# State steps by halves, gate products between them, and a product of two identities behind every half step

## The reference, cut to what matters

```python
# rwkv_branch(z_in, s0_f, s0_b, lp): two directions d over the same tokens
for d in range(2):
    w = -softplus(-(rw_w0[d] + tanh(w_lo) @ rw_w2[d])) - 0.5
    decay = to_heads(exp(-exp(w)))
    a = to_heads(sigmoid(rw_a0[d] + a_lo @ rw_a2[d]))
    kd = kh * (1.0 + (a - 1.0) * k_a)
    y, s_fin = wkv7_scan(rh, decay, kd, vh, -kk, kk * a, s0[d], reverse=(d == 1))
o = ys[0] + ys[1]
o = (o - mean(o)) * rsqrt(var(o) + GN_EPS) * gn_g + gn_b
o = o + bonus[0] + bonus[1]          # then times silu(rw_g)

# gmlp_mix: per chunk of 128 tokens and head
vh = layernorm(gelu(v)) * ln_g + ln_b
mixed = einsum('gpq,bnqgc->bnpgc', w_s, vc) + b_s
out = gelu(u) * mixed                # then times silu(gm_g)

# adaLN: the gate part of mod is needed at the very end only
mod = silu(c) @ ada_w + ada_b;  shift, scale, gate = split(mod, 3)
# attention: rpb is a table of relative position biases, padded into HBM
```

## Time and profile before

| what | value |
|---|---|
| median of 3 runs | 2621.25 us (2617.14 to 2621.5) |
| the profiled execution, its own time | 2618.64 us |
| its span, first to last instruction | 2616.9 us |
| mean granted TensorE clock | 0.944 |
| local stage | about 1266 to 1844 us |
| chain stage, chain | 1844.4 to 1914.0 us |
| chain stage, tail | 1914.0 to 1980.1 us |
| next stage's first instruction | 1983.28 us |

### The profile page before, as it was taken

How to read it: one execution, slowest core, us unless ns; L and a number is a source line. 1 busy time by engine, 2 the same in 40 slices (tenths; PEclk the granted TensorE clock), 3 DMA queues, 4 the chain that set the end, 5 groups by cost and what they waited for, 6 DMA issues and landing times. The chain is left out here.

```text
span 2616.9 us, 65618 instructions
## 1 busy us (share of the span) xinstructions
PE 2262.2 (86%) x26450; PEld 1857.7 (71%) x26450; DVE 1531.4 (59%) x2489; ACT 1020.9 (39%) x1754; POOL 278.3 (11%) x296
## 2 busy tenths in 40 slices
PE   4999999999899999999478877777664995898898
PEld 3788878888788878888366666666563673686687
DVE  5756665667655456666466666655542674776233
ACT  5444244445422134444245555544324664100321
POOL 0000000000000000000410001000232812000421
PEclk7999999999999999999699999999876997898999
DMA  6343323332433333332211111100757006676443
GB/s 225 114 126 117 120 93 113 112 108 93 133 92 99 98 106 107 108 116 96 66 38 38 38 38 48 54 24 24 238 198 230 18 2 202 240 265 221 164 144 120
DMA packets 263877, 300.11 MB, mean 115 GB/s; under 512 B 33274, under 2 KB 203386, under 8 KB 255482
## 3 DMA queue, kind: packets, MB, share of 16 engines
q1 hardware_dynamic: 261370, 288.65, 34.1%
q10 hardware_dynamic: 2304, 8.39, 0.8%
HBM read 194.62 MB, written 102.36 MB: 113 GB/s over the span
## 5 line engine op out<-in xcount | busy, mean ns | idle before, releaser
L715 PE MATMUL proj_ps<-h_hi,w_hi 128*128 128x512 f32 x1656 | 650.4, 393 | 29.1 <-DVE h_lo L465 20.9
L716 PE MATMUL proj_ps<-h_lo,w_hi 128*128 128x512 f32 x1656 | 647.3, 391 | 0.0
L717 PE MATMUL proj_ps<-h_hi,w_lo 128*128 128x512 f32 x1656 | 647.0, 391 | 0.0
L318 ACT CAST w_hi<-w_raw 128x512 fp32r<-128x512 f32 x420 | 255.2, 621 | 696.3 <-PE proj_ps L717 353.5
L715 PEld LDWEIGHTS proj_ps<-h_hi,w_hi 128*128 128x128 f32 x1656 | 312.5, 189 | 99.4 <-issue 27.9
L717 PEld LDWEIGHTS proj_ps<-h_hi,w_lo 128*128 128x128 f32 x1656 | 312.4, 189 | 65.9
L716 PEld LDWEIGHTS proj_ps<-h_lo,w_hi 128*128 128x128 f32 x1656 | 312.7, 189 | 63.5
L482 DVE TENSOR_TENSOR w_lo<-w_raw,w_hi 128x512 fp32r<-128x512 f32 x420 | 283.2, 689 | 44.5 <-ACT w_hi L318 43.8
L498 DVE TENSOR_TENSOR z_slots<-proj_ps,x_rows 128x512 f32<-128x512 f32 x174 | 120.2, 691 | 171.5 <-PE proj_ps L717 169.5
L967 POOL TENSOR_TENSOR neighbours<-z_halo 128x1792 f32<-128x1792 f32 x9 | 28.8, 3201 | 1270.4 <-DMA z_halo<-scratch_zT 1270.4
L498 DVE TENSOR_TENSOR x_rows<-proj_ps,x_rows 128x512 f32<-128x512 f32 x116 | 80.1, 691 | 109.5 <-PE proj_ps L717 103.5
(11 more groups left out here) (329 smaller groups left out, 3912.1 us busy)
## 6 DMA issues: line engine op xcount, KB each, us to landing
w_raw<-in_w_in SPq DMA_DIRECT2D x240, 256.0 KB, 3.0
scratch_gatesT<-z_slots SPq DMA_DIRECT2D x128, 256.0 KB, 2.7
m_gate<-scratch_gatesT SPq DMA_DIRECT2D x32, 1024.0 KB, 5.4
scratch_zT<-z_slots SPq DMA_DIRECT2D x108, 256.0 KB, 2.5
ada<-in_ada_w SPq DMA_DIRECT2D x4, 2048.0 KB, 15.4
mb_raw<-scratch_branchT SPq DMA_DIRECT2D x16, 512.0 KB, 5.4
scratch_mergedT<-m_y SPq DMA_DIRECT2D x8, 1024.0 KB, 5.7
y_raw<-scratch_mergedT SPq DMA_DIRECT2D x16, 512.0 KB, 4.8
```

The source lines that it names most:

```text
L318: A.copy(wh[:, i, :, :], raw[:, q, :, :]).then_inc(w_hi, 1)
L715: T.matmul(out, wh[:, i, k, :], hi[:, o, k, :], start=(first and k == 0), stop=False, skip_group_check=not first)
L716: T.matmul(out, wh[:, i, k, :], lo[:, o, k, :], start=False, stop=False, skip_group_check=not first)
L717: last = T.matmul(out, wl[:, i, k, :], hi[:, o, k, :], start=False, stop=(k == 3), skip_group_check=not first)
```

## The change: what it does

1. `chain_step(i)` is split into `chain_step(i, d)`, one call for each direction, on TensorE and on VectorE. A block now has 16 half steps j. Behind each, TensorE makes one product of `ident` by `ident` (128x128, 128 columns) into the last quarter of bank 5, which nobody reads, and then a piece of other work: a quarter of `turned_rows` (2 products) for j < 4, a quarter of `mixed` (4 products) for 4 <= j < 8, and one product of the gate row for j >= 8. The gate row's 32 products are spread over all four blocks, and `ada` comes in four loads of 1 MB.
2. VectorE's `gated` is split into two halves, and its work is spread over the half steps.
3. In the local stage, direction 1 adds its y to what direction 0 left in `yst` (VectorE, `Ya0.`, `Ya1.`), and `yT` is stored once for a block. GpSimd's sum of the two y is gone, and so is one of the two loads of y for each block.
4. The rpb table is padded and written in the local stage.
5. The tail has a new order on all engines, `mixed(3)` goes behind `outputs(0)`, the gate row is turned at the end, `dev` has three buffers, and odd blocks' outputs use banks 6 and 7. `g` of blocks 0 and 1 is loaded earlier; `g` and y of blocks 2 and 3 are loaded ahead of the stores of the recurrence branch.
6. TensorE waits for `bias_set` before step 3 of the chain, and `ada`'s first load is ahead of the loads of `gm_ln` and `gm_bias` in SyncE's queue.

```diff
@@ local stage, vector
                 for c in range(2):
-                    main_a.after(dve, n, f"Y{c}.{d}")
+                    main_a.after(dve, n, f"Y{c}.0")
+                    if d:
+                        y = yst[:].rearrange("p m (g c t) -> p c g m t", g=2, c=2)[:, c]
+                        done(V.tensor_tensor(y, ps[:, 4 + c, 256:512].rearrange("p (g m t) -> p g m t", g=2, m=2), y, ALU.add), f"Ya{c}.")
@@ chain stage, sync
             load_v(0)
...
             load_ug(0)
+            load_ada(0)
             for n, name in enumerate(("gm_ln_g", "gm_ln_b")):
...
             load_v(1)
             load_ug(1)
-            load_ada(0)
+            load_g(0)
...
             load_v(2)
             load_ug(2)
-            sp.wait_ge(rpb_in, 16)
-            src = pad[:].rearrange("r (a c) -> r a c", a=1).to_broadcast([4 * NDR, GRID, 2 * GRID - 1])
-            sp.dma_start(t["rpbPad"][:, :, 0:2 * GRID - 1], src).then_inc(pad_out, 16)
-            gm_v.after(sp, 0, "m")
+            load_ada(1)
+            load_g(1)
+            gm_v.after(sp, 0, "m1")
             store(0, 0, 0)
             load_v(3)
             load_ug(3)
-            load_g(0)
-            load_g(1)
-            load_ada(1)
-            gm_v.after(sp, 1, "m")
+            load_ada(2)
+            gm_v.after(sp, 1, "m1")
             store(0, 1, 1)
             load_y(0)
             load_gates(0)
-            gm_v.after(sp, 2, "m")
+            load_ada(3)
+            gm_v.after(sp, 2, "m1")
             store(0, 2, 2)
             load_y(1)
             load_gates(1)
-            gm_v.after(sp, 3, "m")
+            load_g(2)
+            load_y(2)
+            gm_v.after(sp, 3, "m1")
             store(0, 3, 3)
+            load_g(3)
+            load_y(3)
             for b in range(NB):
-                if b + 2 < NB:
-                    load_g(b + 2)
-                    load_y(b + 2)
                 rw_v.after(sp, b, "out")
                 store(4, b, NB + b)
                 if b + 2 < NB:
                     load_gates(b + 2)
@@ chain stage, tensor
+            pe.wait_ge(bias_set, 2)
             for b in range(NB):
-                for k in range(EACH):
-                    chain_step(1 + AHEAD + b * EACH + k)
-                    if k < 2:
-                        turned_rows(b, k)
-                    elif k < 4 and b:
-                        mixed(b - 1, k - 2)
-                    elif k == 5 and b in (1, 3):
-                        gate(b // 2)
-            pe.wait_ge(gate_row, 1)
...
+                for j in range(2 * EACH):
+                    chain_step(1 + AHEAD + b * EACH + j // 2, j % 2)
+                    T.matmul(ps[:, 5, 3 * P:4 * P], s["ident"][:], s["ident"][:], start=True, stop=True)
+                    if j < 4:
+                        turned_rows(b, j)
+                    elif j < 8 and b:
+                        mixed(b - 1, (j - 4) // 2, j % 2)
+                    elif j >= 8:
+                        gate(b, j - 8)
+            pe.wait_ge(s_done, 4 * (STEPS + 1))
...
             outputs(0)
+            for p in range(2):
+                mixed(NB - 1, p, 0)
+                mixed(NB - 1, p, 1)
             outputs(1)
             statistics(0)
             outputs(2)
             statistics(1)
+            outputs(3)
             root_columns(0)
-            outputs(3)
+            statistics(2)
             root_columns(1)
-            statistics(2)
+            statistics(3)
             root_columns(2)
-            statistics(3)
             root_columns(3)
@@ chain stage, vector
+                for j in range(2 * EACH):
+                    chain_step(1 + AHEAD + b * EACH + j // 2, j % 2)
+                    if j in (4, 6):
+                        squares_sum(b, (j - 4) // 2)
+                    if j == 7:
...
+                        seed(lambda ins, name: gm_n.own(dve, b, ins, name), sums[:], EPS, b)
+                    if j in (8, 9) and b:
+                        scaled(b - 1, j - 8)
+                    if j in (10, 11) and b:
+                        gated(b - 1, j - 10)
+                    if j >= 14:
+                        normed(b, j - 14)
```

More of the change, by code:

```diff
@@ L1439, in unit @@
                         main_g.after(pe, n, f"Z.{d}")
-                        before(main_a, "Y1.")
+                        if d:
+                            main_a.after(pe, n, "Y1.0")
+                        else:
+                            main_v.earlier(pe, n, "Ya1.1")
                         before(main_v, "Q1.")
@@ L1735, in turned_rows, with chain_step @@
-            def turned_rows(b, r):
-                if r == 0:
-                    gm_in_a.after(pe, b, "v")
-                gm_n.earlier(pe, b, f"rows{r}")
-                for c in range(2 * r, 2 * r + 2):
-                    for p in range(2):
-                        at = (c % 2) * BR + p * P
-                        last = T.matmul(ps[:, r, at:at + P], gin[:, b % 2, 2 + p, c * P:(c + 1) * P], chain["centre"][:], start=True, stop=True)
-                gm_p.done(last, f"rows{r}")
-            def mixed(b, p):
-                gm_n.after(pe, b, "rows1")
-                gm_v.earlier(pe, b, f"s{p}")
-                for c in range(NCK):
+            def chain_step(i, d):
+                pe.wait_ge(s_done, 4 * (i - 1) + 2 * d + 2)
+                for p in range(2):
+                    for h in range(2):
+                        last = T.matmul(ps[half(h), 6 + d, p * CH:(p + 1) * CH], chain["P"][half(h), d, chunk(d, i), p, :],
+                                        state(d, p, i)[half(h), :], start=True, stop=True)
+                last.then_inc(p_done, 1)
@@ new lines, in turned_rows @@
+            def turned_rows(b, c):
+                r = c // 2
+                if c == 0:
+                    gm_in_a.after(pe, b, "v")
+                if c % 2 == 0:
+                    gm_n.earlier(pe, b, f"rows{r}")
+                for p in range(2):
+                    at = (c % 2) * BR + p * P
+                    last = T.matmul(ps[:, r, at:at + P], gin[:, b % 2, 2 + p, c * P:(c + 1) * P], chain["centre"][:], start=True, stop=True)
+                if c % 2:
+                    gm_p.done(last, f"rows{r}")
@@ L1749, in mixed @@
+            def mixed(b, p, part):
+                if part == 0:
+                    gm_n.after(pe, b, "rows1")
+                    gm_v.earlier(pe, b, f"s{p}")
+                for c in range(2 * part, 2 * part + 2):
                     for g in (2 * p, 2 * p + 1):
                         last = T.matmul(ps[half(g % 2), 2 + p, c * P:(c + 1) * P], rows[:, c, g * CH:(g + 1) * CH], wt[:, g, :], start=True, stop=True)
-                mix_p.done(last, f"mixed{p}")
-            def gate(n):
-                pe.wait_ge(ada_in, 16 * n + 16)
-                for k in range(4):
-                    for j in range(4):
-                        last = T.matmul(ps[32 * j:32 * j + 32, 4, 0:2 * P], gsc[:, 4 * n + k, :], ada[:, k, j * 2 * P:(j + 1) * 2 * P],
-                                        start=(n == 0 and k == 0), stop=True, skip_group_check=True)
-                last.then_inc(gate_ps, 1)
@@ L1761, in _, with gate @@
-            chain_step(1)
+                if part:
+                    mix_p.done(last, f"mixed{p}")
+            def gate(n, i):
+                k, j = divmod(i, 4)
+                if i == 0:
+                    pe.wait_ge(ada_in, 16 * n + 16)
+                last = T.matmul(ps[32 * j:32 * j + 32, 4, 0:2 * P], gsc[:, 2 * n + k, :], ada[:, k, j * 2 * P:(j + 1) * 2 * P],
+                                start=(n == 0 and k == 0), stop=True, skip_group_check=True)
+                if i == 7:
+                    last.then_inc(gate_ps, 1)
@@ L1792, in outputs @@
                         rw_o.after(pe, b - 2, f"o{p}")
-                    elif b == 1:
-                        gm_v.after(pe, NB - 1, f"s{p}")
+                    elif b == 0:
+                        gm_n.after(pe, NB - 1, f"rows{p}")
                     for c in range(8):
```

195 lines of the change are left out of this document (89 added, 106 removed).

## The result

The kernel after takes 2633.53 us (median of 18 runs, 2627.04 to 2640.96), the kernel before 2621.66 beside it (18 runs). The ratio is 1.0047, 95% interval 1.0037 to 1.0057: slower, where the forecast was 2609.0 us and faster. 2633.5 also lies above the range.

The account below looks back on a forecast made before the run. Chain blocks were taken as TensorE-bound in their first half, VectorE-bound in their second, the tail as a row of waits. 2618.6 + 4.5 (chain) + 0.5 (local stage) - 14.6 (tail) = 2609.0 us; range 2603 to 2616.

Parts of the forecast that it names:

- The loop: Chain stage's four blocks of half steps: 61.3 us at full clock against some 59 before, so about 2 us longer.
- price of a gate product: Gate-row product on TensorE in a block's second half: 0.12 us each, leaving TensorE's 5.6 us under VectorE's 6.72.
- Rival B: Chain loop: two more tile-shape changes on TensorE in 32 half steps, 0.17 us each, +10.9 us, 2620; chance 0.13.
- Rival A: Chain loop: clock falls despite the fill; +10 us for a quarter at half clock, some +40 for all; chance 0.10.
- Rival C: Blocks 1 to 3: TensorE waits at j = 8 for late `ada`, 1 to 3 us a block, 2617; chance 0.09.
- The head and the cold start: Chain's start: TensorE's bias wait 0.5, later bias loads 1, first steps at half clock 1.8 us; counted as 2.5.
- The tail: From the loop's end to the chain stage's end: 51.5 us against 66.1, a gain of 14.6.
- the prediction's other tail: Chain stage's tail at half clock throughout: 56.5 us, a gain of 9.6, kernel at 2614.
- The local stage: VectorE's added work in direction 1 makes `inv_first` 0.3 us later, mostly covered by PQ's products; taken as +0.5 us.

Follow-up runs that it names:

- e2: The changed kernel without the 64 products of two identities; 2612.87 us, ratio 0.9985 to the kernel before.
- e4: The changed kernel with whole steps, no identity products, a block's eight gate products in one go; 2607.26 us, ratio 0.9959 to the kernel before.
- e3: The changed kernel with gate products issued four at a time and no identity products; 2614.71 us, ratio 0.9993 to the kernel before.
- e10: As e8, but `g` of blocks 0 and 1 loaded behind u and g of block 3; 2603.89 us, ratio 0.9939 to the kernel before.
- e8: As e4, but bias loaded before `ada` and no TensorE wait for it; 2601.35 us, 2601.14 when run again; ratios 0.9937 and 0.9927 to before.
- e1: The changed kernel with gate products four at a time, behind half steps 8 and 12; 2618.56 us, ratio 1.0004 to the kernel before.
- e9: As e1, but ordered so that two and two neighbouring gate products use the same 32 columns; 2627.95 us, one run.
- e5: As e4, plus an identity product behind each block's last four steps, 16 in all; 2607.21 us, ratio 0.9950 to the kernel before.
- e7: The changed kernel with each identity product 64x64 in place of 128x128; 2619.42 us, ratio 1.0002 to the kernel before.

## Why the prediction was wrong

**The loop is the step that failed**, forecast 61.3 us, measured 85.70. The price that failed first is that of a gate product, "1.93 / 16 = 0.12": an average over a group in which four products ran side by side. Alone it is 0.55. With that price the second half of a block is 8 x (0.305 + 0.27 + 0.55) = 9.0 us on TensorE, above VectorE's 7.0, and the bound changes engine. The rest are the fixed parts of a group: the same two shapes were priced at 0.305 for half a chain step and 0.27 for the identity product, and took 0.38 and 0.42. In us above the forecast:

| half steps | forecast | measured | too much |
|---|---|---|---|
| gate, blocks 1 to 3 | 24 x 0.875 | 24 x 1.345 | 11.3 |
| gate, block 0 | 8 x 0.71 | 8 x 1.345 | 5.1 |
| first four of block 0 | 4.5 | 7.6 | 3.1 |
| `turned_rows`, other blocks | 12 x 1.12 | 12 x 1.245 | 1.5 |
| `mixed` | 12 x 1.10 | 12 x 1.385 | 3.4 |

That is 24.4; the four half steps of block 0 that have none of the three took 0.2 less than forecast, so 24.2 of the 24.4 us by which the loop is longer.

By cause: the gate product's price alone would have made the gate half steps 0.305 + 0.27 + 0.55 = 1.125 us, 9.3 us over the forecast (24 x 0.25 + 8 x 0.415). The fixed parts add 32 x 0.22 = 7.0 in the same half steps and 4.9 in the others, the cold start 3.1. So the step that failed has two mis-sized terms, and the fixed parts, though small each, are the larger one in sum.

**Rival B** priced a change of shape at 0 to 0.2 us, for two more changes in the half steps with j < 8 only, and had a chance of 0.13. The runs put the price inside these bounds. From groups of two sizes in e2, e4 and after, a group costs its products plus a fixed part between other shapes: chain 0.38 for four products and 0.61 for eight, so 0.15 fixed; `turned_rows` 0.64 and 1.09, so 0.19; `mixed` 0.59 and 1.03, so 0.15; gate 0.56 and 0.99 for one round and two, so 0.13. What the rival missed is the number of groups, above all in the second half of the blocks, where I had let VectorE cover them. It was the right mechanism beside the wrong bound.

**Rival A** (the clock falls in the loop) did not come: 0.96. The Trainium skill (TensorE: Matmul & The Clock Gate, its table of goals) lays a fall to idle gaps; this loop had no gap and no fall, so the trace agrees. The row does not cover the fall in the kernel before, where no wait of TensorE ahead of it was above 1.34 us. Without the fill the clock was lower, 0.89 in e2 and 0.80 in e3, but in e2 this cost less than the fill.

**Rival C** (late `ada`) did not come in the kernel after, whose long loop gave the transfers time (146 GB/s). It came in the shorter loops without fill: 1.39 us in e2, 0.75 and 1.36 in e3, 0.54 in e4, 5.54 in e10 (there behind 2 MB of `g`).

**The head and the cold start** were counted at 2.5 us together, and are 3.5 and 3.1. VectorE waits for the bias 3.2 us longer than before, beyond the upper bound of 2.5; e8, which takes back the order of the loads and TensorE's wait, has a head of 10.31 us against 12.85. The head ends with VectorE's instruction on the bias, which waited for a transfer, and TensorE's new wait stands behind that instruction; so the rows lay the head to the loads, and the wait can cost only what comes after it. No run has the one edit without the other.

**The tail** was right: forecast 51.5 and a gain of 14.6, measured 49.57 and 16.6. TensorE ran through its outputs with no wait for `g`, and ScalarE's wait for the last gate's load stood in the chain at the end, as forecast. Outputs of blocks 2 and 3 took 5.4 and 3.95 us where I had 5.5 each. The Trainium skill (TensorE: Matmul & The Clock Gate, Part 4) says that transposes do not count as busy for the clock, and by that the prediction's other tail was 56.5 us. It did not come out that way, but no run here separates the transposes.

**The local stage** was forecast at +0.5 us and took 1.1 less; no experiment says which of its edits did it.

So the change has a part that gains 17 us (tail and loads) and a part that loses 30 (half steps, fill, head). With the second undone (e8) the kernel is faster than before by 0.63 to 0.73%, more than the 0.4% that the forecast had promised for the whole.

## What to carry to other kernels

Never divide a group's time by its count where the products lie side by side in different columns of the array (e1 and e9; rows were not tried): price a lone one by a whole round of the array. Add a fixed part for each group between groups of another shape; with the fp32 shapes of this kernel it was 0.13 to 0.19 us. Before an engine is given filler because another is the bound, write its half steps out with those prices. A higher clock is worth only what the work under it loses without it; here 0.89 against 0.96 was far cheaper than 64 products.

## What the runs showed of the hardware

A lone fp32 product of 128x32 by 256 columns takes 0.55 us at the full clock, four in different column groups 0.56, two pairs in the same groups 0.99. A 128x128 by 128 identity product takes 0.22 us behind its own shape, 0.33 behind 64x64, and 0.42 with another change behind it.

VectorE stood 4.0 to 4.9 us in four kernels (e3, e4, e5 and both executions of e8), in block 1 at the sums or the states behind them, with its operands ready, while transfers ran at over 400 GB/s; with 1 MB fewer in that burst the gap was 2.0 and 2.1 us. I take it for its own instructions arriving behind the data. The packet of an instruction queue 1.5 to 2.0 us ahead of the end of every one of these gaps fits that, but the profile does not say whose instructions it carries, and no run moved it by itself. What is shown is that the gap shrinks with the burst. Before has no such gap, nor have the kernels with longer loops; at the same place, with its operands ready, VectorE stood 0.99 us in e7 and 1.33 in e2.
